# A decoder layer on one core: a halved first piece, constant matmuls at the start, an earlier weight split and rounded prefix sums

## What is computed

```python
x = x + 0.5 * _swiglu(_rmsnorm(x, ffn1_norm[l]), ffn1_w_gate[l], ffn1_w_up[l], ffn1_w_down[l])
u = _rmsnorm(x, mix_norm[l]) @ w_in[l]
...
# stick-breaking heads, per block of 128 queries
z = jnp.einsum('bqhd,bkhd->bhqk', q[:, t0:t1], k[:, :t1]).astype(jnp.float32) * scale
log_1m_beta = jnp.where(mask, jax.nn.log_sigmoid(-z), 0.0)
tail = lax.cumsum(log_1m_beta, axis=3, reverse=True) - log_1m_beta
a = jnp.where(mask, jnp.exp(jax.nn.log_sigmoid(z) + tail), 0.0)
...
x = x + jnp.concatenate([a_out, b_out], axis=-1) @ w_out[l]
x = x + 0.5 * _swiglu(_rmsnorm(x, ffn2_norm[l]), ffn2_w_gate[l], ffn2_w_up[l], ffn2_w_down[l])
x = _rmsnorm(x, final_norm[l])
```

## Time and profile before

| | us |
|---|---|
| runs | 1893.20, 1893.87, 10671.68 |
| median | 1893.87 |
| the profiled execution | 1893.42 |
| its span | 1891.6 |
| TensorE busy in it | 1875.1 (99%) |
| VectorE busy | 1133.5 (60%) |
| ScalarE busy | 902.9 (48%) |
| DMA engines, mean share | 57% |

### The profile page before, as it was taken

One profiled execution on the slowest core, in us unless ns is written; L12 is line 12 of the kernel. 1 busy time (PEld: TensorE's weight loads), 2 busy tenths in 40 slices (PEclk: granted clock), 3 DMA queues, 4 the chain that ended last, 5 costly groups with the idle time before them and its releaser, 6 DMA issues.

```text
span 1891.6 us, 28251 instructions
## 1 busy us (share of the span) xinstructions
PE 1875.1 (99%) x10792; PEld 1638.4 (87%) x10792; DVE 1133.5 (60%) x1303; ACT 902.9 (48%) x1213; POOL 16.7 (1%) x18
## 2 busy tenths in 40 slices
PE   8999999999999999999999999999999999999998
PEld 7888888888888888888888888888888888888887
DVE  7665556555555667565655566655555565556565
ACT  7444434444344446554656455444344444344454
POOL 0000000000000000100000000000000000000000
PEclk9999999999999999999999999999999999999999
DMA  9555655555555556554445555556555556655553
GB/s 306 180 197 181 197 178 195 184 197 180 181 196 186 186 167 216 179 173 162 157 161 172 172 185 180 197 182 196 178 195 183 197 179 187 191 192 185 176 172 119
DMA packets 344098, 349.91 MB, mean 185 GB/s; under 512 B 5984, under 2 KB 342112, under 8 KB 344032
## 3 DMA queue, kind: packets, MB, share of 16 engines
q1 hardware_dynamic: 343456, 348.02, 56.6%
q10 hardware_dynamic: 576, 0.96, 0.1%
HBM read 346.85 MB, written 2.10 MB: 184 GB/s over the span
## 4 chain that ended last, share of the span: by engine, by line
PE 61%; issue 38%; DVE 0%; DMA 0%; ACT 0%; POOLq 0%; POOL 0%; DVEq 0%
PE psum L1164 38%; PE psum L1169 19%; PE psum L1250 1%; PE psum L1253 0%; PE psum L1402 0%; DVE x_res L1118 0%; DMA param_sb<-in_params 0%; PE psum L1336 0%; PE psum L1347 0%; PE psum L1362 0%; PE psum L1393 0%; PE psum L1201 0%; PE psum L1394 0%; PE psum L1363 0%; PE psum L1346 0%
## 5 line engine op out<-in xcount | busy, mean ns | idle before, releaser
L1164 PE MATMUL psum<-x_split,w_split 128*128 128x512 f32 x3008 | 931.7, 395 | 0.0
L726 DVE TENSOR_TENSOR w_split<-w_raw,w_split 128x1024 fp32r<-128x1024 f32 (+1 forms) x664 | 766.5, 1196 | 252.3 <-ACT w_split L442 246.6
L442 ACT ACTIVATE w_split<-w_raw 128x1024 fp32r<-128x1024 f32 (+1 forms) x664 | 651.3, 1030 | 320.2 <-PE psum L1169 318.8
L1169 PEld LDWEIGHTS psum<-x_split,w_split 128*128 128x128 f32 x3008 | 551.8, 188 | 124.8
L1169 PE MATMUL psum<-x_split,w_split 128*128 128x256 f32 x3008 | 578.0, 279 | 0.0
L1164 PE MATMUL psum<-h_split,w_split 128*128 128x512 f32 x1640 | 507.1, 395 | 0.0
L1164 PEld LDWEIGHTS psum<-x_split,w_split 128*128 128x128 f32 x3008 | 465.4, 189 | 8.1
L1169 PEld LDWEIGHTS psum<-h_split,w_split 128*128 128x128 f32 x1640 | 300.4, 188 | 67.7
L450 ACT ACTIVATE lo_sum<-psum 128x512 f32<-128x512 f32 x159 | 95.0, 597 | 507.1 <-PE psum L1164 507.1
L1169 PE MATMUL psum<-h_split,w_split 128*128 128x256 f32 x1640 | 314.6, 279 | 0.0
L1164 PEld LDWEIGHTS psum<-h_split,w_split 128*128 128x128 f32 x1640 | 254.0, 189 | 4.8
(11 more groups left out here) (140 smaller groups left out, 530.9 us busy)
## 6 DMA issues: line engine op xcount, KB each, us to landing
w_raw<-in_ffn_gate SPq DMA_DIRECT2D x86, 1024.0 KB, 5.0
w_raw<-in_ffn_up SPq DMA_DIRECT2D x86, 1024.0 KB, 5.0
w_raw<-in_ffn_down SPq DMA_DIRECT2D x64, 1024.0 KB, 5.5
w_raw<-in_w_in SPq DMA_DIRECT2D x48, 1024.0 KB, 5.2
w_raw<-in_ffn_down SPq DMA_DIRECT2D x32, 768.0 KB, 4.8
w_raw<-in_w_out SPq DMA_DIRECT2D x16, 1024.0 KB, 5.5
x_res<-in_x_t SPq DMA_DIRECT2D x8, 256.0 KB, 6.9
w_raw<-in_ffn_gate SPq DMA_DIRECT2D x8, 256.0 KB, 7.0
```

The source lines that it names most:

```text
L442: nc.scalar.activation(w_split[:, slot % 2, 0, h * half:(h + 1) * half], w_raw[:, slot, h * half:(h + 1) * half], ACT.Copy).then_inc(hi_ma ...
L726: nc.vector.tensor_tensor(w_split[:, slot % 2, 1, part], w_raw[:, slot, part], w_split[:, slot % 2, 0, part].bitcast(F32), ALU.subtract).t ...
L1164: return mm(psum[:, 2 * j + b, :], one, other, start=first, stop=last)
L1169: return mm(psum[:, 2 * j + b, 256:512], one, other, start=False, stop=False)
```

## The change

It has four parts.

1. The first strip of x and the first gate and up pieces are brought and split in two halves, one block of 128 rows each (`first_landed`, `first_hi`, `first_lo`), and TensorE starts on the first half. Two small operations on parameters go behind the first body on VectorE.
2. Three float32 matmuls of constants (512 columns each) stand ahead of TensorE's first wait.
3. Around the end of the first body: on ScalarE two squares stay in front, then the first half of chunk 4's high parts, then the other six squares, then the rest; the preload of the Silu table goes behind the copies. On VectorE the additions of squares are interleaved with the low parts of chunk 4. On TensorE `norm(0)` goes from ahead of chunk 4 to behind it, and `norm_spread(0)` from ahead of chunk 5 to behind it, which is just ahead of chunk 6.
4. `sb_sums` takes float32r operands: `softplus` is written as high and low parts (a Copy on ScalarE, a subtraction on VectorE, both over 128x768, one chunk after the scores), the triangle and the ones are copied to a float32r tile once, and each head takes four float32r matmuls (384, 128, 128, 384 columns) in place of two float32 ones. `rope_gain` shares `head_out`.

```diff
@@ sync
-                    for st in range(NS):
+                    for k in range(2):
+                        done = first_landed if k == 0 else (x_landed[0], entry_landed(0, 0)[0], entry_landed(0, 1)[0])
+                        sp.dma_start(x_res[:, 0, k, :], x_t[:, k, :]).then_inc(done[0], 16)
+                        for w in range(2):
+                            sp.dma_start(w_raw[:, 2 * w, k * STRIP:(k + 1) * STRIP], source(0, 2 * w)[:, k, :]).then_inc(done[1 + w], 16)
+                    for st in range(1, NS):
@@ scalar
+            act.wait_ge(first_landed[0], 16)
+            first_x_hi(0, first_hi, 1)
+            for w in range(2):
+                act.wait_ge(first_landed[1 + w], 16)
+                first_w_hi(w, 0, first_hi)
...
-            for st in range(NS):
-                nc.scalar.activation(first_squares[st], x_res[:, st, :, :], ACT.Square).then_inc(first_squared, 1)
-            nc.scalar.activation(warm[:, 0:1], param_sb[:, 0:1], ACT.Silu)
+            for st in range(2):
+                first_square(st)
...
                     if at_first and i == 0:
-                        hi_parts(4, 1, 0, kn)
+                        hi_parts(4, 1, 0, kn, halves=(0,))
+                        for st in range(2, NS):
+                            first_square(st)
+                        hi_parts(4, 1, 0, kn, halves=(1,))
+                        hi_parts(5, 1, 1, kn)
                         copy_lo(0, 0, 1.0, bank=6)
-                        hi_parts(5, 1, 1, kn)
                         copy_lo(1, 1, 1.0)
+                        nc.scalar.activation(warm[:, 0:1], param_sb[:, 0:1], ACT.Silu)
...
+                def sb_soft_high(p):
+                    act.wait_ge(sb_soft, 2 * p + 2)
+                    nc.scalar.activation(soft_split[:, 0, :, :], softplus, ACT.Copy).then_inc(sb_soft_hi, 1)
@@ vector
                     if at_first and i == 0:
-                        lo_parts(4, 0, kn)
+                        add_first_square(1)
+                        lo_parts(4, 0, kn, halves=(0,))
+                        for st in range(2, 5):
+                            add_first_square(st)
+                        lo_parts(4, 0, kn, halves=(1,))
+                        for st in range(5, NS):
+                            add_first_square(st)
+                        lo_parts(5, 1, kn, halves=(0,))
                         add_halves(0, 0, bank=6)
+                        lo_parts(5, 1, kn, halves=(1,))
                         norm_means(0)
-                        lo_parts(5, 1, kn, halves=(0,))
+                        add_halves(1, 1)
                         norm_diagonal(0)
-                        lo_parts(5, 1, kn, halves=(1,))
-                        add_halves(1, 1)
...
+                def sb_soft_low(p):
+                    dve.wait_ge(sb_soft_hi, p + 1)
+                    nc.vector.tensor_tensor(soft_split[:, 1, :, :], softplus, soft_split[:, 0, :, :].bitcast(F32),
+                                            ALU.subtract).then_inc(sb_soft_lo, 1)
@@ tensor
+            one = nc.const_aps.tensor(1.0, (P, 1))
+            for _ in range(3):
+                mm(psum[:, 5, :], one.broadcast_to([P, P]), one.broadcast_to([P, 512]), start=True, stop=True)
...
                         first_body()
-                        norm(0)
                         return
...
                     if at_first:
+                        norm(0)
+                    chunk(2 * s + 1, 1, 0, ph["kn"], True, x_block(1), block_ready=ready[1], by_half=at_first)
+                    if at_first:
                         pe.wait_ge(psum_freed, freed_value(0))
                         norm_spread(0)
-                    chunk(2 * s + 1, 1, 0, ph["kn"], True, x_block(1), block_ready=ready[1], by_half=at_first)
...
-                pe.wait_ge(sb_soft, 2 * p + 2)
+                pe.wait_ge(sum_weights_made, 2)
+                pe.wait_ge(sb_soft_lo, p + 1)
                 wait_banks("sb_sums", p)
                 for h in range(2):
-                    mm(psum[:, 6 + h, 0:384], const("tri"), softplus[:, h, :], start=True, stop=False)
-                    ins = mm(psum[:, 6 + h, P:T], const("ones"), softplus[:, h, T:384], start=False, stop=True)
+                    mm(psum[:, 6 + h, 0:384], sum_weights[:, 0, :], soft_split[:, 0, h, :], start=True, stop=False)
+                    mm(psum[:, 6 + h, P:T], sum_weights[:, 1, :], soft_split[:, 0, h, T:384], start=False, stop=False)
+                    mm(psum[:, 6 + h, P:T], sum_weights[:, 1, :], soft_split[:, 1, h, T:384], start=False, stop=False)
+                    ins = mm(psum[:, 6 + h, 0:384], sum_weights[:, 0, :], soft_split[:, 1, h, :], start=False, stop=True)
```

More of the change, by code:

```diff
@@ L218, in hybrid_layer @@
         quarter_landed = [[sem(f"quarter_landed{j}{q}") for q in range(3)] for j in range(RAW_SLOTS)]
+        first_landed = [sem(f"first_landed{n}") for n in range(3)]
+        first_hi = sem("first_hi")
+        first_lo = sem("first_lo")
         entry_hi = sem("entry_hi")
@@ L438, in hi_parts @@
                 half = kn * STRIP // 2
-                for h in range(2):
+                for h in halves:
                     if after_entry and h:
@@ L477, in _, with first_x_hi, first_w_hi @@
             act.wait_ge(params_landed, 16)
-            for st in range(NS):
+            def first_x_hi(k, done, step):
+                nc.scalar.activation(x_split[:, 0, k, 0, :], x_res[:, 0, k, :], ACT.Copy,
+                                     scale=gain_by_strip[:, 0, 0, k:k + 1]).then_inc(done, step)
+            def first_w_hi(w, k, done):
+                cols = slice(k * STRIP, (k + 1) * STRIP)
+                nc.scalar.activation(w_split[:, w, 0, cols], w_raw[:, 2 * w, cols], ACT.Copy).then_inc(done, 1)
+            act.wait_ge(first_landed[0], 16)
[3 more added lines that the diff above has]
+                first_w_hi(w, 0, first_hi)
+            act.wait_ge(x_landed[0], 16)
+            first_x_hi(1, x_hi_made, 1)
+            for w in range(2):
+                act.wait_ge(*entry_landed(0, w))
+                first_w_hi(w, 1, entry_hi)
+            for st in range(1, NS):
                 act.wait_ge(x_landed[st], 16)
@@ L679, in mix @@
                         after[cc].append((sb_logs, n))
+                        after[cc + 1].append((sb_soft_high, n))
                     if kind == "sb_sums":
@@ L783, in _, with first_x_lo, first_w_lo @@
             dve.wait_ge(params_landed, 16)
[L784 to L787 removed]
+            def first_x_lo(k, done):
+                stt(x_split[:, 0, k, 1, :], x_res[:, 0, k, :], gain_by_strip[:, 0, 0, k:k + 1],
+                    x_split[:, 0, k, 0, :].bitcast(F32), ALU.mult, ALU.subtract).then_inc(done, 1)
+            def first_w_lo(w, k, done):
+                cols = slice(k * STRIP, (k + 1) * STRIP)
+                nc.vector.tensor_tensor(w_split[:, w, 1, cols], w_raw[:, 2 * w, cols], w_split[:, w, 0, cols].bitcast(F32),
+                                        ALU.subtract).then_inc(done, 1)
+            dve.wait_ge(first_hi, 1)
+            first_x_lo(0, first_lo)
+            for w in range(2):
+                dve.wait_ge(first_hi, 2 + w)
+                first_w_lo(w, 0, first_lo)
+            dve.wait_ge(x_hi_made, 1)
+            first_x_lo(1, x_ready)
+            for w in range(2):
+                dve.wait_ge(*entry_hi_made(0, w))
+                first_w_lo(w, 1, entry_lo)
+            for st in range(1, NS):
                 x_lo_parts(st, st, 0)
@@ L795, in _, with add_first_square @@
                                             w_split[:, w, 0, cols].bitcast(F32), ALU.subtract).then_inc(signal, step)
-            for st in range(1, NS):
+            def add_first_square(st):
                 dve.wait_ge(first_squared, st + 1)
@@ L813, in prepare @@
                 nc.vector.memset(rest_gain[0:32, :], 1.0).then_inc(prepared, 1)
+                for n, name in enumerate(("tri", "ones")):
+                    nc.vector.tensor_copy(sum_weights[:, n, :], const(name)).then_inc(sum_weights_made, 1)
             def copy_rope():
@@ L1060, in mix @@
                         after[cc].append((sb_softplus, n))
+                        after[cc + 1].append((sb_soft_low, n))
                     if kind == "sb_sums":
@@ L1235, in first_body @@
                 def first_body():
-                    for st in range(NS):
-                        pe.wait_ge(x_ready, st + 1)
+                    pieces = [(0, (0,)), (0, (1,))] + [(st, (0, 1)) for st in range(1, NS)]
+                    for st, ks in pieces:
+                        if (st, ks) != (0, (0,)):
+                            pe.wait_ge(x_ready, st + 1)
                         for w in range(2):
-                            pe.wait_ge(*entry_lo_made[(st, w)])
+                            if (st, ks) == (0, (0,)):
+                                pe.wait_ge(first_lo, 2 + w)
+                            else:
+                                pe.wait_ge(*entry_lo_made[(st, w)])
```

(2 more changed lines are left out.)

20 lines of the change are left out of this document (13 added, 7 removed).

## The result

| | before | after |
|---|---|---|
| median of the runs, us | 1893.71 (14 runs) | 1898.33 (14 runs, 1897.18 to 1899.82) |
| ratio | | 1.0024 [1.0017, 1.0031] |
| the profiled execution, us | 1893.42 | 1899.62 |
| its span, us | 1891.6 | 1897.8 |

The changed kernel is 4.6 us slower. That is far within the 2% that the forecast gave as its measure, and in the range of 1893.5 to 1899.5, but it is twice the +2.3 us of the forecast's sum. The range is 6 us wide and takes in the kernel before (1893.71) too, so lying in it says little on whether the mechanism was right. Three of the 14 executions before lie far off the others (the highest is 10671.68); the ratio leaves them out.

The account below looks back on a forecast made before the run. TensorE, busy 1875.1 of 1891.6 us, was taken as the bound. Parts 1 to 3 cost +4.2 us, the sums save 2.4, new waits add 0.5: +2.3, forecast 1896.0 us, range 1893.5 to 1899.5.

Parts of the forecast that it names:

- Part 1: At the start, halved first pieces let TensorE start at about 6.3 us: a lead of 1.1 us, 0.4 kept.
- The allowed 0.7 us of waiting: At the start, TensorE's wait for the next strip, whose transfers come at the old rate: 0.7 us.
- Part 2: At the start, constant matmuls end by 6.3 us, hold up nothing and raise the lead to 1.9 us.
- Here the lead is spent: Around chunk 4, the early start's lead is lost, since chunk 4's data land at 27.3 us as before.
- the 1.5 us: At the start, time ten matmuls lose at half clock; the constants would save it, but it wasn't counted as gain.
- Part 3: Around chunk 4, the new order makes chunk 7 start 4.2 us later; parts 1 to 3 sum to +4.2 us.
- The pause of 3.6 us: Between the spread and chunk 6, TensorE stands still about 3.6 us for VectorE's copy, scaling and low parts.
- Part 4: In the sums, float32r saves 0.6 us each, -2.4 us over four; new waits for the splits cost +0.5 us.
- the third rival: At chunk 4's landing, the lead survives and the kernel is faster; 1892.9 us with a landing 1.6 us earlier; chance 0.07.
- The clock fell in this pause: Ahead of chunk 6, a rival: the idle pause drops the clock to half, 1896.8 us, up to 1898; chance 0.2.
- Narrow float32r matmuls do gain: In the sums, the rival claimed the opposite: 128 columns take 0.22 us, saving 0.6 not 2.4, 1897.8 us; chance 0.25.
- the change does what it says: Behind the spread, the rival claimed the opposite: VectorE isn't held and the wait stays short, 1892 us; chance 0.03.

Follow-up runs that it names:

- experiment 3: Changed kernel without the three constant matmuls at the start: 1898.15 us, ratio 1.0023 to the kernel before.
- experiment 2: Changed kernel with part 1 undone: 1896.68 us; with only its first transfers made whole: 1896.9; with the 640 KB constants' transfer behind chunk 7: 1897.23.
- Part 1 undone: Changed kernel with whole first pieces in transfers and splitting, parts 2 to 4 kept: 1896.68 us, ratio 1.0017 to the kernel before.
- the order: Kernel before with part 3 only (squares, norm and spread moved): 1899.62 us, ratio 1.003.
- parts 1 and 2 alone: Kernel before with halved first pieces and constant matmuls, old order and float32 sums: 1893.98 us, ratio 0.9998.
- experiment 5: Changed kernel, whole first pieces, late constants' transfer, chunks 6 to 8 split ahead: 1889.72 us; split by halves: 1889.96; kernel before with sums, constant matmuls, late transfer: 1890.45.
- the filled pause: Changed kernel with three float32 constant matmuls put behind the spread, into TensorE's pause ahead of chunk 6: 1897.64 us, ratio 1.0019.

## Why the prediction was right, and where it was off

**Part 1.** "ScalarE starts at 4.80 us when the parameters land, and that doesn't move" was wrong: with the small transfers the parameters land in 2.5 us and not in 4.0, and ScalarE starts at 3.29. So "TensorE starts at about 6.3 us" was too late, and the split chain would have let it start at 4.82. The allowed 0.7 us of waiting became 1.46 us ahead of 10.83 us, since the second strip's x lands later too: ScalarE waits 0.90 us for it, until 8.26.

**Part 2.** That the constants "hold up nothing" was wrong: at half clock they run to about 6.2 us, and products ready at 4.8 stood behind them, the second until 6.62. It was harmless, by experiment 3, because the landing decides. "Here the lead is spent" was right, and so was not counting the 1.5 us. The Trainium skill (TensorE: Matmul & The Clock Gate, "Why this matters for your kernels") advises a warm-up ahead of a measurement. Used as an optimization, such a warm-up was worth nothing here, where a transfer sets the next start, as experiment 3 shows.

**Part 3.** This is the step that failed: chunk 4 "lands at 27.3 us", with 0.3 us as the allowance for a later landing. It lands at 29.5. The prediction looked at what could make it earlier and priced what could make it later at 0.3 us for more pieces. Three issues more at the 0.47 us that SyncE's timeline shows for each are 1.4 us by themselves, and 128 KB in that time is less than the 346 GB/s that the transfers ran at from 4 to 6 us in the kernel before. In experiment 2 the term measured 1.8 to 2.0 us on the landing and 1.4 to 1.65 us of the median.

The chain behind it was right to within 0.25 us, once the landing is near what was assumed (27.5 us). Part 1 undone against the forecast: chunk 4 29.9 (29.7), its second half 33.98 (33.8), chunk 6 47.53 (47.3); the median 1896.68 (1896.0). The pause of 3.6 us, ended by VectorE's low part, is there, 3.60. That VectorE is late for chunk 7 as well showed when the clock no longer hid it (0.6 us for 0.7).

**Part 4.** One sum "1.14 us": measured 1.14. "A new wait of about 0.4 us" for p = 2: 0.38. For p = 1 0.1 was allowed: none. -2.4 + 0.4 is -2.0; alone it measured -1.7. Two of the four sums took 1.22 and 1.23 us and not 1.14, which is 0.17 us of the 0.3 between.

**The sum.** 1893.42 + 2.3 + 0.45 is 1896.2, not the 1896.0 that was written; 1896.0 is +2.3 on the median of 1893.71. The 1892.9 of the third rival should be 1893.3 by its own terms.

**Rivals.** The clock fell in this pause or shortly behind it in every profile that had it; the mechanism was named, at 0.2, and it should have been in the sum: 0.7 us of the median, 1.8 in the profiled execution. Narrow float32r matmuls do gain. The lead didn't survive: the landing would have had to be 1.1 us earlier and was 2.2 later. VectorE's order did hold the copy of `rstd` and the low parts behind the spread, so the change does what it says.

The account of +4.6 us: the forecast's +2.3; the landing, 1.4 to 1.65; the clock, 0.7. That is 4.4 to 4.65. The last two are differences of medians that were measured; the +2.3 is the forecast's own sum and no measurement: the kernel with part 1 undone came in at +2.9 with the clock fallen in its profile, which less 0.7 is 2.2. The forecast was right in direction and in the pause that it named as the main cost, and its time held because the range had room for two terms that were left out or too small and that both made the kernel slower.

## What to carry to other kernels

Find what the lead of an earlier start runs into before counting it: if the next stage begins with a transfer, only an earlier landing helps, and here cutting the first three transfers in two made it 1.8 to 2.0 us later. When an instruction is moved on one engine, look at what the engines that answer it have queued between its result and the next thing that the first one needs: here moving two chunks' splits ahead on VectorE and ScalarE was worth 4.7 us. Try parts of a change alone, since one that pays (the sums, -1.7) can be buried under one that doesn't (the order, +5.8 alone). Then undo them one by one in the whole as well: part 1 cost 0.2 us by itself with the constants and 1.65 in company.

## What the hardware showed

- Around each pause of 3.6 us the granted clock went to half (1.2 GHz), in all six profiled kernels that had it: in two of them inside the pause and for 6.8 us, in four between 0.1 and 1.35 us behind its end and for 3.4 us. In one more (parts 1 and 2 alone) it went to half behind two waits of 0.8 and 0.4 us (0.63 and 0.16 in the rows' brackets) around eight matmuls of one column; no run tests what made it fall there. Six constant passes in 2.75 us kept it up, though 1.0 us of waiting followed.
- The kernel before has two groups of runs as well. Of its 33 runs beside experiment 5, 20 take 1893.1 to 1893.9 us with a mean granted clock of 0.998, and 13 take 1894.6 to 1895.4 with 0.997. Its profile is of the first kind, and where the clock falls in the others is not known.
- At the start the stretches give the granted clock as 1.00 while matmuls take twice their later time: six constant passes take 0.86 us each there and 0.43 in the filled pause. At the start the clock has to be read from durations, not from that column.
- A float32r matmul of 128 columns took 0.06 us in one place and 0.11 in the next (L1493 and L1494), one of 384 columns 0.17 and 0.23, in rows that differ in what stands ahead of and behind them; narrow ones do gain, but not evenly.
- With six pieces of 128 KB first, the stretches from 4 to 10 us moved 203, 261 and 292 GB/s; with three of 256 KB in their place, 321, 335 and 347.
